# Second layer's lag matrices and phase tables made earlier, decays in two buffers

## Chip, cores and metric

One NeuronCore of a Trainium2 chip runs the whole program. The metric is the device time of one execution in microseconds. The kernel before took 1739.98 us in the median of three runs (1738.82 to 1740.71).

## What is computed

The reference is a trunk of two layers over 528 tokens (16 meta tokens and 512 others) of width 1024. Each layer has a mixer with two branches, and behind it a feed-forward part: dense SwiGLU in the first layer, top-2-of-8 experts in the second. The change touches the S5 branch of the mixer, a diagonal complex recurrence of 64 states for each of 32 groups of 16 channels:

```python
for layer in range(DEPTH):
    z = rmsnorm(hs, mix_norm[layer]) @ w_in[layer]
    # s5_branch: per group 16 inputs drive 64 complex states
    bu = einsum('btgh,gph->btgp', u, bb)          # bb from lambda, dt, B
    s  = associative_scan(s[t] = ab * s[t-1] + bu[t])
    y  = Re(einsum('btgp,ghp->btgh', s, c)) + d * u
    y_a = (gelu(y) * sigmoid(gelu(y) @ w_glu + b)) @ w_proj
    # rglru_branch: conv, gates, a real scan
    hs = hs + (gates0 * y_a + gates1 * y_b) @ w_out[layer]
    hs = hs + (swiglu if layer == 0 else moe_swiglu)(rmsnorm(hs, ffn_norm[layer]))
return rmsnorm(hs, final_norm)
```

## The kernel before

All activations lie feature by token in SBUF. TensorE (PE) multiplies in units: one unit is a 128x1024 slab of weights, split by ScalarE (ACT, `split_hi`) and VectorE (DVE, `split_lo`, tile `wl`) into a high and a low part, so that each product is three matmuls. A mixer has 28 such units for `w_in` (`U_IN`), then those of the GLU, the merge and the output. The order on every engine is written out by hand; engines meet at semaphores.

The S5 recurrence is done in chunks of 8 tokens. The 32 groups go in 8 batches of 4 (`NB`, `GB`), and a batch has three parts, one behind each of three units of `w_in`, from the fourth on (`slot_of`; here P1, P2 and P3):

- P1 (L1841 to L1851) turns the **lag matrices** `m1t` of the batch into the matrices of the chunk. Behind it ACT copies `m1`, and DVE makes `m3` (L1289) and `m2` (semaphore `m2_ready`).
- P2 (L1861) gives each chunk's input to the states, into `side`. Behind it DVE runs the **rotation**: it turns the states by the **phase table** of the batch (`rot`), runs a real scan with the **decays** (L1315, `turned<-decay,rot`), and turns back (`state`, semaphore `rot_ready`).
- P3 (L1868, L1869) gives the batch's outputs from `m3`, `m2` and `state`. It waits for the rotation.

So PE has one unit between P2 and P3 in which DVE must do the rotation, and one unit between P1 and P2.

GpSimd (POOL) makes what DVE and PE need for that. For every batch b of either layer it does, in this order (L608 to L662):

```python
if done:
    pool.wait_ge(p1_done, done)        # P1 of batch b-1
    pool.wait_ge(m2_ready, done)       # m2 of batch b-1
...                                    # fetch pbuf of b+1; lag matrices m1t
if done > 1:
    pool.wait_ge(rot_ready, done - 1)  # rotation of batch b-2
...                                    # phase table: a copy and 24 tensor_tensor
if done:
    pool.wait_ge(rot_ready, done)      # rotation of batch b-1
g.tensor_copy(decay[:, :, 1:NC], col1(mag8)).then_inc(tab_ready, 1)
```

`m1t` and `decay` have one buffer, `phases` and the parameters `pbuf` two. The lag matrices take seven instructions, of which L631, the L537 behind it and L634 are 128x512; the table doubles its columns six times with four `tensor_tensor` each (L653, L537, L655, L656). In the second layer, POOL first waits for the dense part's last residual (`hs_at_norm[2]`, L599), fetches `gw` and `pbuf`, and starts with batch 0. Ahead of that, at the end of the first mixer, it fills two DRAM buffers of the expert part with zeros (`zero`, L590 to L596) and then waits for the whole dense part. The dense part works in units like the mixer's; its tiles `gt`, `ft`, `fh`, `fl` are written by ACT and DVE.

In the second mixer, units of the gates need only 512 tokens. At two places of each mixer (`PAIR_AT`) DVE has in addition the RG-LRU's products and scans on 128x1056 tiles (`ii`, `xc`, `th`, `gg`), behind the rotations of batches 3 and 6.

## Time and profile before

| | us |
|---|---|
| median of three runs | 1739.98 |
| profiled execution, its own time | 1742.03 |
| its span | 1740.4 |
| PE busy | 1645.2 (95%) |
| VectorE busy | 1021.3 (59%) |
| ScalarE busy | 778.3 (45%) |
| GpSimd busy | 371.8 (21%) |
| mean granted TensorE clock | 0.977 of full |

The span is that of the profiled execution, from its first to its last instruction; what lies around it is 1.6 us. Stages by the timeline: first mixer to about 355 us, dense part to 796 us, second mixer to about 1140 us, router and experts behind it. A time in a profile row is counted from the span's start; the number behind it is how long the row's instructions took, and what stands in brackets is how long the engine had been idle and who released it.

### The profile page before, as it was taken

The page shows a single profiled execution, that of the slowest core. Times are in us where ns is not written, and L with a number is a line of the kernel's source. Part 1 is how long each engine was busy: PE and PEld are TensorE (multiplying, and loading weights), DVE is VectorE, ACT ScalarE, POOL GpSimd, SP SyncE. Part 2 cuts the span into 40 slices and gives each one's busy share as a digit, 9 for nine tenths or more (in the row PEclk, how much of TensorE's full clock was granted, in tenths as well). Part 3 has the DMA queues.
Part 4 walks back from the last instruction along what each step waited for, and adds up shares of the span by engine and source line. Part 5 has one row for each costly group of instructions (what it writes and reads, how often), then busy time and mean ns, then how long its engine had stood idle before and what let it go on. Part 6 is the DMA issues. An engine that isn't in the chain of part 4 may idle for free. (4 is left out here: it accounts for less than half of the span.)

```text
span 1740.4 us, 26958 instructions
## 1 busy us (share of the span) xinstructions
PE 1645.2 (95%) x10652; PEld 1466.3 (84%) x10652; DVE 1021.3 (59%) x1286; ACT 778.3 (45%) x947; POOL 371.8 (21%) x662
## 2 busy tenths in 40 slices
PE   5899999989999999998999999979999999999992
PEld 5799999989999999998987878757788777777872
DVE  6868477443333233324766676368547766866985
ACT  4354473332221222223353563247446755755773
POOL 7688630020000000004677700020000000000001
PEclk9899999989999999998999999989999999999996
DMA  4522224373232232324532234069658967966994
GB/s 162 119 82 89 82 80 134 99 291 109 84 97 85 86 95 85 96 86 145 115 91 81 83 99 153 13 247 411 245 185 297 339 236 245 376 243 229 369 371 159
DMA packets 99444, 291.24 MB, mean 167 GB/s; under 512 B 27376, under 2 KB 27504, under 8 KB 99200
## 3 DMA queue, kind: packets, MB, share of 16 engines
q1 hardware_dynamic: 84624, 245.43, 41.8%
q0 software_dynamic: 9504, 33.60, 5.4%
q10 hardware_dynamic: 5200, 10.64, 1.9%
q8 instruction: 75, 1.23, 0.3%
q14 instruction: 41, 0.34, 0.1%
HBM read 261.39 MB, written 28.24 MB: 166 GB/s over the span
## 5 line engine op out<-in xcount | busy, mean ns | idle before, releaser
L1157 DVE TENSOR_TENSOR mwl<-mraw,mwh 128x1024 fp32r<-128x1024 f32 x288 | 337.8, 1220 | 73.1 <-ACT mwh L1052 72.1
L1743 PE MATMUL acc<-xh,wh 128*128 128x264 f32 (+1 forms) x1560 | 368.1, 306 | 3.4 <-DVE xl L1157 1.8
L1743 PE MATMUL acc<-xl,wh 128*128 128x264 f32 (+1 forms) x1560 | 360.3, 301 | 0.0
L1743 PE MATMUL acc<-xh,wl 128*128 128x264 f32 (+1 forms) x1560 | 359.3, 300 | 0.0
L1157 DVE TENSOR_TENSOR wl<-raw,wh 128x1024 fp32r<-128x1024 f32 x164 | 203.6, 1242 | 206.0 <-ACT wh L744 205.6
L1052 ACT ACTIVATE mwh<-mraw 128x1024 fp32r<-128x1024 f32 x288 | 288.5, 1053 | 61.9 <-PE acc L2014 32.8
L1743 PEld LDWEIGHTS acc<-xh,wh 128*128 128x128 f32 x1560 | 251.2, 189 | 17.2 <-issue 3.3
L1743 PEld LDWEIGHTS acc<-xl,wh 128*128 128x128 f32 x1560 | 250.2, 189 | 8.7
L1743 PEld LDWEIGHTS acc<-xh,wl 128*128 128x128 f32 x1560 | 249.7, 189 | 9.3
L744 ACT ACTIVATE wh<-raw 128x1024 fp32r<-128x1024 f32 x164 | 172.5, 1052 | 153.1 <-PE acc L1743 149.6
L2012 PE MATMUL acc<-mwh,xth 128*128 128x512 f32 x432 | 171.3, 396 | 7.9 <-ACT ytok L1118 5.4
L2013 PE MATMUL acc<-mwh,xtl 128*128 128x512 f32 x432 | 168.9, 391 | 0.0
L2014 PE MATMUL acc<-mwl,xth 128*128 128x512 f32 x432 | 168.8, 391 | 0.0
L701 POOL DMA_DIRECT2D yg_d<-ytok x11 | 6.0, 541 | 522.3 <-ACT ytok L1118 518.6
L2012 PEld LDWEIGHTS acc<-mwh,xth 128*128 128x128 f32 x432 | 81.5, 189 | 27.3 <-DVE mwl L1157 6.5
L2014 PEld LDWEIGHTS acc<-mwl,xth 128*128 128x128 f32 x432 | 81.4, 189 | 17.5
L2013 PEld LDWEIGHTS acc<-mwh,xtl 128*128 128x128 f32 x432 | 81.6, 189 | 16.4
L601 POOL DMA_DIRECT2D gw<-in_wg x2 | 1.1, 546 | 425.5 <-DVE hs L1411 425.5
L2012 PE MATMUL acc<-mwh,hth 128*128 128x512 f32 x216 | 85.9, 398 | 0.0
L2014 PE MATMUL acc<-mwl,hth 128*128 128x512 f32 x216 | 84.3, 390 | 0.0
L2013 PE MATMUL acc<-mwh,htl 128*128 128x512 f32 x216 | 84.2, 390 | 0.0
L1743 PE MATMUL acc<-fh,wh 128*128 128x264 f32 x384 | 78.8, 286 | 0.0
(412 smaller groups left out, 2661.4 us busy)
## 6 DMA issues: line engine op xcount, KB each, us to landing
mraw<-in_W SPq DMA_DIRECT2D x288, 512.0 KB, 5.6
raw<-in_W SPq DMA_DIRECT2D x164, 512.0 KB, 3.5
xg_d<-zero POOLq DMA_DIRECT2D x15, 512.0 KB, 9.9
yg_d<-ytok POOLq DMA_DIRECT2D x9, 512.0 KB, 4.9
xt<-xg_d POOLq DMA_DIRECT2D x8, 512.0 KB, 8.1
pbuf<-in_s5m POOLq DMA_DIRECT2D x16, 192.0 KB, 3.1
yg_d<-zero POOLq DMA_DIRECT2D x5, 512.0 KB, 20.9
hs<-in_xT SPq DMA_DIRECT2D x8, 264.0 KB, 8.2
```

What stands on the lines that cost most here:

```text
L601: pool.dma_start(gw[:, r, :, :], wg[l, :, r, :, :]).then_inc(wg_landed, 16)
L701: pool.dma_start(rows(yg_d, BASE[ORDER[b]] + t * TOK, n), ytok[0:n, (tb + t) % 2, :])\
L744: a.activation(wh[s][:, :], raw[s][:, :], ACT.Copy).then_inc(hi_ready[s], 1)
L1052: a.activation(mwh[w][:, :], mraw[j % RAWS][:, :], ACT.Copy).then_inc(wide_hi, 1)
L1157: return v.tensor_tensor(out, a, b, op)
L1743: ins = mm(out, w, x[:, t0:t1], start=first and i == 0, stop=last and i == 2)
L2012: mm(out, hi, mwh[w][:, cols], start=first, stop=False)
L2013: mm(out, lo, mwh[w][:, cols], start=False, stop=False)
L2014: return mm(out, hi, mwl[w][:, cols], start=False, stop=last)
```

## The change

- **Second layer, batches 0 and 1**: their lag matrices, phase tables and decays are made during the dense part, behind the writes of zeros, in tiles that are idle then (`early_m1t`, `early_phase`, with work tiles and a small fetch `early_pbuf` of their own). PE and DVE read these tiles for the two batches (`lags_of`, `phase_of`). `pbuf` of both batches is still fetched after the dense part, since P1 and `m2` need the rest of it; PE waits for it, and for the zeros in `tapsT`, at P1 of these two batches.
- **Second layer, batches 2 and 3**: their tables are made at the second mixer's start and behind `m2` of batch 0, ahead of their lag matrices.
- **Second layer, batches 4 to 7**: table b starts as soon as the rotation of b-2 is done, ahead of the lag matrices of b, which still wait for P1 and `m2` of b-1.
- **Decays** are in two buffers, in a place of their own; decays b wait for the rotation of b-2 and not of b-1.
- **First layer**: the order stays lags, table, decays; only the decays' wait for the rotation of b-1 goes.

The core of the diff:

```diff
@@ placements @@
-        decay = place("decay", [P, GB, NC], at=f)
+        f = [LR()[0] + 4 * 12 * T, LR()[1]]
+        early_phase = [place(f"early_phase{b}", [P, 2, GB, NC], at=f) for b in range(2)]
+        f = [LR()[0] + 4 * 3 * T, LR()[1]]
+        early_m1t = [place("early_m1t0", [P, GB, P], at=f)]
+        f = [LR()[0] + 4 * 4 * T, LR()[1]]
+        early_pbuf = place("early_pbuf", [P, 2, 2, GB * GC], at=f)
+        early_pt1 = place("early_pt1", [P, GB * P], at=f)
+        early_pt2 = place("early_pt2", [P, GB * P], at=f)
+        early_bx = place("early_bx", [P, GB, GC], at=f)
+        early_by = place("early_by", [P, GB, GC], at=f)
+        f = [LR()[0] + 4 * 7 * T, LR()[1]]
+        early_m1t.append(place("early_m1t1", [P, GB, P], at=f))
+        decay = place("decay", [P, 2, GB, NC])
+        def early(l, b):
+            return l and b < 2
+        def lags_of(l, b):
+            return early_m1t[b] if early(l, b) else m1t
+        def phase_of(l, b):
+            return early_phase[b] if early(l, b) else phases[:, b % 2]
...
@@ GpSimd: the loop that goes @@
-            for l in range(LAYERS):
-                if l:
-                    pool.wait_ge(hs_ready, hs_at_norm[1])
-                    link(g.memset(zero[:, :], 0.0))
...
-                    pool.wait_ge(zeroed, ZDMAS * 16)
-                    pool.wait_ge(hs_ready, hs_at_norm[2])
...
-                link(g.memset(phases[:, :, 0, :, 0:1], 1.0))
-                link(g.memset(phases[:, :, 1, :, 0:1], 0.0))
-                link(g.memset(tapsT[:, 0:PADW - P], 0.0))
-                link(g.memset(decay[:, :, 0:1], 0.0))
-                for b in range(NB):
...
-                    pool.wait_ge(pb_landed[b % 2], 16 * (l * NB // 2 + b // 2 + 1))
-                    if done:
-                        pool.wait_ge(p1_done, done)
-                        pool.wait_ge(m2_ready, done)
-                    if 0 < b < NB - 1:
-                        pool.dma_start(pbuf[:, (b + 1) % 2, :, :], s5m[l, b + 1, :, :, :])\
-                            .then_inc(pb_landed[(b + 1) % 2], 16)
...
-                    g.tensor_tensor(m1t[:, :, :].rearrange("p g (j h) -> p g j h", h=GC), by_group(pt1), by_group(pt2),
...
-                    phase = phases[:, b % 2]
-                    if done > 1:
-                        pool.wait_ge(rot_ready, done - 1)
...
-                    pool.wait_ge(m1t_ready, done + 1)
-                    link(g.tensor_copy(phase[:, :, :, 1], turn[:, :, 0, gs]))
...
-                    if done:
-                        pool.wait_ge(rot_ready, done)
...
-                    g.tensor_copy(decay[:, :, 1:NC], col1(mag8)).then_inc(tab_ready, 1)
-                    pool.wait_ge(tab_ready, done + 1)
...
@@ GpSimd: what takes its place @@
+            def lags(l, b):
...
+                p1, p2, x, y = (early_pt1, early_pt2, early_bx, early_by) if early(l, b) else (pt1, pt2, bx, by)
+                bb = (early_pbuf if early(l, b) else pbuf)[:, b % 2, 0:2, :].rearrange("p t (g h) -> p t g h", g=GB)
...
+                g.tensor_tensor(lags_of(l, b)[:, :, :].rearrange("p g (j h) -> p g j h", h=GC), by_group(p1), by_group(p2),
+                                ALU.add).then_inc(m1t_ready, 1)
+                pool.wait_ge(m1t_ready, n + 1)
+            def phase_table(l, b):
...
+                p1, p2 = (early_pt1, early_pt2) if early(l, b) else (pt1, pt2)
+                phase = phase_of(l, b)
...
+                link(g.tensor_copy(phase[:, :, :, 1], turn[:, :, 0, gs]))
...
+                    link(g.tensor_tensor(phase[:, 1, :, k:k + c], z1[:, 1, :, :], z2[:, 0, :, :], ALU.add))
+            def decays(l, b):
+                n = l * NB + b
+                gs = slice(l * GROUPS + b * GB, l * GROUPS + (b + 1) * GB)
+                g.tensor_copy(decay[:, b % 2, :, 1:NC], mag8[:, gs].unsqueeze(2).to_broadcast([P, GB, NC - 1]))\
+                    .then_inc(tab_ready, 1)
+                pool.wait_ge(tab_ready, n + 1)
+            def free_batch(l, b):
+                pool.wait_ge(p1_done, l * NB + b)
+                pool.wait_ge(m2_ready, l * NB + b)
+                if 0 < b < NB - 1:
+                    pool.dma_start(pbuf[:, (b + 1) % 2, :, :], s5m[l, b + 1, :, :, :])\
+                        .then_inc(pb_landed[(b + 1) % 2], 16)
+            def unit_phases(phase):
+                link(g.memset(phase[:, 0, :, 0:1], 1.0))
+                link(g.memset(phase[:, 1, :, 0:1], 0.0))
+            link(g.memset(decay[:, :, :, 0:1], 0.0))
+            for b in range(2):
+                unit_phases(phases[:, b])
+            link(g.memset(tapsT[:, 0:PADW - P], 0.0))
+            for b in range(NB):
+                pool.wait_ge(pb_landed[b % 2], 16 * (b // 2 + 1))
+                if b:
+                    free_batch(0, b)
+                lags(0, b)
+                if b > 1:
+                    pool.wait_ge(rot_ready, b - 1)
+                phase_table(0, b)
+                decays(0, b)
+            pool.wait_ge(hs_ready, hs_at_norm[1])
+            for b in range(2):
+                pool.dma_start(early_pbuf[:, b, :, :], s5m[1, b, :, 0:2, :]).then_inc(early_landed, 16)
+            link(g.memset(zero[:, :], 0.0))
+            for z in range(0, SLOTS, P):
+                n = min(P, SLOTS - z)
+                pool.dma_start(xg_d[z:z + n, :], zero[0:n, :]).then_inc(zeroed, 16)
+            for z in range(FIRST_EXTRA, SLOTS, P):
+                n = min(P, SLOTS - z)
+                pool.dma_start(yg_d[z:z + n, :], zero[0:n, :]).then_inc(zeroed, 16)
+            pool.wait_ge(zeroed, ZDMAS * 16)
+            pool.wait_ge(early_landed, 16 * 2)
+            pool.wait_ge(rot_ready, NB)
+            for b in range(2):
+                lags(1, b)
+                unit_phases(early_phase[b])
+                phase_table(1, b)
+                decays(1, b)
+            pool.wait_ge(hs_ready, hs_at_norm[2])
+            for r in range(2):
+                pool.dma_start(gw[:, r, :, :], wg[1, :, r, :, :]).then_inc(wg_landed, 16)
+            for b in range(2):
+                pool.dma_start(pbuf[:, b, :, :], s5m[1, b, :, :, :]).then_inc(pb_landed[b], 16)
+            g.memset(tapsT[:, 0:PADW - P], 0.0).then_inc(taps_zeroed, 1)
+            for b in range(2):
+                unit_phases(phases[:, b])
+            phase_table(1, 2)
+            free_batch(1, 1)
+            phase_table(1, 3)
+            for b in range(2, NB):
+                n = NB + b
+                if b > 3:
+                    pool.wait_ge(rot_ready, n - 1)
+                    phase_table(1, b)
+                pool.wait_ge(rot_ready, n - 1)
+                decays(1, b)
+                pool.wait_ge(pb_landed[b % 2], 16 * (NB // 2 + b // 2 + 1))
+                free_batch(1, b)
+                lags(1, b)
...
@@ VectorE, TensorE @@
-                        phase = phases[:, b % 2]
+                        phase = phase_of(l, b)
...
-                        link(v.tensor_tensor_scan(flat(turned), flat(decay), flat(rot), 0.0, ALU.mult, ALU.add))
+                        link(v.tensor_tensor_scan(flat(turned), flat(decay[:, b % 2]), flat(rot), 0.0, ALU.mult, ALU.add))
...
+                        lag = lags_of(l, b)
+                        if early(l, b):
+                            pe.wait_ge(pb_landed[b], 16 * (NB // 2 + 1))
+                            pe.wait_ge(taps_zeroed, 1)
```

The change moves instructions on POOL alone. Its rows at two places follow, as the programs have them, with the semaphores that each waits for. First the end of the first mixer's work: before, POOL goes from the writes of zeros (`zero`) to the fetches that wait for the dense part's end (`gw`, `pbuf`).

```order
L590 MEMSET zero 128x1024 [waits hs_ready,tab_ready]
L593 DMA xg_d<-zero 128x1024 [waits pool_chain]
L593 DMA xg_d<-zero 128x1024 x14
L596 DMA yg_d<-zero 128x1024 x5
L601 DMA gw<-in_wg 128x512 [waits hs_ready,zeroed]
L601 DMA gw<-in_wg 128x512
L603 DMA pbuf<-in_s5m 128x384 x2
L604 MEMSET phases 128x2x4
```

Now, from the writes of zeros on, the first lag matrices of the second layer follow, behind `zeroed` (`early_pt_113` and `early_pt_114` are the work tiles `early_pt1` and `early_pt2`):

```order
L696 DMA early_pbuf<-in_s5m 128x128 [waits hs_ready,tab_ready]
L696 DMA early_pbuf<-in_s5m 128x128
L697 MEMSET zero 128x1024
L700 DMA xg_d<-zero 128x1024 [waits pool_chain]
L700 DMA xg_d<-zero 128x1024 x14
L703 DMA yg_d<-zero 128x1024 x5
L621 TENSOR_TENSOR early_pt_113<-cfr,early_pbuf 128x128 [waits rot_ready,early_landed,zeroed]
L562 TENSOR_TENSOR early_pt_113<-cfi,early_pbuf 128x128
L623 TENSOR_TENSOR early_bx<-early_pt_113 128x64 [waits pool_chain]
L562 TENSOR_TENSOR early_by<-early_pt_113 128x64
L629 TENSOR_TENSOR early_pt_113<-apr,early_bx 128x512 [waits pool_chain]
L562 TENSOR_TENSOR early_pt_114<-api,early_by 128x512
```

Two fetches stand ahead of the zeros, and everything for batches 0 and 1 stands between the zeros and the fetch of `gw`.

Then the second layer around batch 5, whose lag matrices are the `m1t` row. Before, the two rows on top end the table of batch 4, the decays are those of batch 4, and the last row starts the table of batch 5:

```order
L655 TENSOR_TENSOR phases<-pt_85,pt_86 128x4x2 [waits pool_chain]
L656 TENSOR_TENSOR phases<-pt_85,pt_86 128x4x2
L661 COPY decay<-mag_143 128x4x65 [waits rot_ready,pool_chain]
L620 DMA pbuf<-in_s5m 128x384 [waits p1_done,m2_ready,pb_landed1,tab_ready]
L623 TENSOR_TENSOR pt_85<-cfr,pbuf 128x128
L537 TENSOR_TENSOR pt_85<-cfi,pbuf 128x128
L625 TENSOR_TENSOR bx<-pt_85 128x64 [waits pool_chain]
L537 TENSOR_TENSOR by<-pt_85 128x64
L631 TENSOR_TENSOR pt_85<-apr,bx 128x512 [waits pool_chain]
L537 TENSOR_TENSOR pt_86<-api,by 128x512
L634 TENSOR_TENSOR m1t<-pt_85,pt_86 128x512 [waits pool_chain]
L643 COPY phases<-turn 128x8 [waits m1t_ready,rot_ready]
```

Now the two rows on top end the table of batch 5, the decays are those of batch 5, and the last row starts the table of batch 6:

```order
L656 TENSOR_TENSOR phases<-pt_84,pt_85 128x4x2 [waits pool_chain]
L657 TENSOR_TENSOR phases<-pt_84,pt_85 128x4x2
L663 COPY decay<-mag_151 128x4x65 [waits rot_ready,pool_chain]
L672 DMA pbuf<-in_s5m 128x384 [waits p1_done,m2_ready,pb_landed1,tab_ready]
L621 TENSOR_TENSOR pt_84<-cfr,pbuf 128x128
L562 TENSOR_TENSOR pt_84<-cfi,pbuf 128x128
L623 TENSOR_TENSOR bx<-pt_84 128x64 [waits pool_chain]
L562 TENSOR_TENSOR by<-pt_84 128x64
L629 TENSOR_TENSOR pt_84<-apr,bx 128x512 [waits pool_chain]
L562 TENSOR_TENSOR pt_85<-api,by 128x512
L632 TENSOR_TENSOR m1t<-pt_84,pt_85 128x512 [waits pool_chain]
L644 COPY phases<-turn 128x8 [waits rot_ready,m1t_ready]
```

Between two sets of lag matrices there is one table as before, but it is the next batch's table; the lag matrices stay behind the same `p1_done` and `m2_ready`.

## Rows read from the trace of the kernel before

**Rows 1.** Waits: engine, line, waited for; us in total, times, longest.

```profile
PE side L1868 <- DVE state L1157: 9.2, 5, 3.5
DVE rot L1157 <- POOL decay L661: 3.7, 5, 1.3
```

**Rows 2.** Timeline of PE, second mixer, batches 2, 4 and 7: start, us, instruction.

```profile
884.12 1.00 PE L1861 MATMUL side<-uu,m 128*128 128x66 f32 x8
...
890.60 0.33 PE L1868 MATMUL side<-uu,m 128*128 128x66 f32 x2
...
898.93 0.63 PE L1841 MATMUL side<-m1t,pbuf 128*32 128x128 f32 x8
...
928.81 1.00 PE L1861 MATMUL side<-uu,m 128*128 128x66 f32 x8
...
938.41 0.69 PE L1868 MATMUL side<-uu,m 128*128 128x66 f32 x2 [2.98 <-DVE state L1157]
...
949.91 0.63 PE L1841 MATMUL side<-m1t,pbuf 128*32 128x128 f32 x8
...
1001.82 1.00 PE L1861 MATMUL side<-uu,m 128*128 128x66 f32 x8
...
1009.49 0.44 PE L1868 MATMUL side<-uu,m 128*128 128x66 f32 x2 [1.04 <-DVE state L1157]
```

**Rows 3.** Windows: stretch, length, PE busy (matmuls), granted clock, DMA share, GB/s.

```profile
172.00:174.00 2.00, 2.00 (x16) 1.00 0.68 170
939.00:945.00 6.00, 6.00 (x23) 0.51 0.35 98
```

**Rows 4.** Timeline of PE, first mixer, batches 0 and 4.

```profile
72.32 0.70 PE L1868 MATMUL side<-uu,m 128*128 128x66 f32 x2 [3.51 <-DVE state L1157]
...
170.46 0.44 PE L1868 MATMUL side<-uu,m 128*128 128x66 f32 x2 [1.49 <-DVE state L1157]
```

**Rows 5.** Timeline of DVE, second mixer: end of rotation 3, rotation 4.

```profile
912.41 0.48 DVE L1157 TENSOR_TENSOR state<-state,rot 128x260 f32<-128x260 f32 x1
...
929.44 1.23 DVE L1157 TENSOR_TENSOR wl<-raw,wh 128x1024 fp32r<-128x1024 f32 x1
931.47 1.32 DVE L1157 TENSOR_TENSOR rot<-side,phases 128x264 f32<-128x264 f32 x3 [0.79 <-POOL decay L661]
...
934.56 2.39 DVE L1157 TENSOR_TENSOR rot<-turned,phases 64x260 f32<-64x260 f32 x2
936.98 1.37 DVE L1157 TENSOR_TENSOR state<-state,rot 128x260 f32<-128x260 f32 x1
```

**Rows 6.** Timeline of POOL, second mixer: table and decays 4, lags 5, table 5.

```profile
910.61 0.43 POOL L643 COPY phases<-turn 128x8 f32<-128x8 f32 x1
...
930.96 0.40 POOL L661 COPY decay<-mag 128x260 f32<-128x260 f32 x1
...
934.28 1.18 POOL L631 TENSOR_TENSOR pt<-apr,bx 128x512 f32<-128x512 f32 x1
...
936.74 1.32 POOL L634 TENSOR_TENSOR m1t<-pt,pt 128x512 f32<-128x512 f32 x1
938.20 0.21 POOL L643 COPY phases<-turn 128x8 f32<-128x8 f32 x1
...
947.91 0.40 POOL L661 COPY decay<-mag 128x260 f32<-128x260 f32 x1
```

**Rows 7.** Timeline of DVE, second mixer, rotation of batch 7, first and last step.

```profile
1005.11 1.32 DVE L1157 TENSOR_TENSOR rot<-side,phases 128x264 f32<-128x264 f32 x3 [0.63 <-POOL decay L661]
...
1009.01 0.43 DVE L1157 TENSOR_TENSOR state<-state,rot 128x260 f32<-128x260 f32 x1
```

**Rows 8.** Timelines of the dense part: DVE, then ACT, then POOL's next instruction.

```profile
399.76 1.23 DVE L1157 TENSOR_TENSOR wl<-raw,wh 128x1024 fp32r<-128x1024 f32 x1 [3.56 <-ACT wh L744]
404.13 0.70 DVE L1157 TENSOR_TENSOR ft<-gt,acc 128x528 f32<-128x528 f32 x1 [3.15 <-PE acc L1743]
```

```profile
409.92 0.61 ACT L977 ACTIVATE gt<-acc 128x528 f32<-128x528 f32 x1 [3.20 <-PE acc L1743]
```

```profile
796.17 1.08 POOL L601 DMA_DIRECT2D gw<-in_wg  x2 [425.47 <-DVE hs L1411]
```

84 lines of the change are left out of this document (36 added, 48 removed).

## The prediction

> **What bounds the kernel now.** PE is the engine that sets the time, so I read its waits first. In the S5 parts only one wait of PE has a cost: P3 waits for DVE's rotation, five times, 9.2 us in all, and DVE waits for POOL's decays five times, 3.7 us in all [rows 1]. PE's timeline says where the five are. In the first mixer 3.51 us (batch 0) and 1.49 us (batch 4) [rows 4], in the second 2.98 us (batch 4) and 1.04 us (batch 7) [rows 2]; that leaves 9.2 - 9.02, some 0.2 us, for the fifth. Nowhere does PE wait for lag matrices.
>
> The windows add a second cost. In the 6 us behind the wait of 2.98 us the granted clock is 0.51, near the lower of its two levels (1.2 and 2.4 GHz) [rows 3]. Behind the wait of 1.49 us it is 1.00 [rows 3]. So one long pause has a price that goes on after it.
>
> Then I follow the chain from P3 back. In batch 4 of the second mixer DVE has ended its weight split at 929.44 + 1.23 = 930.67, and starts the rotation only at 931.47, 0.79 us later, released by the decays [rows 5]. The decays come at 930.96 because they stand behind a table that took from 910.61 to 930.96, 20.35 us [rows 6]. The next table took 947.91 - 938.20 = 9.71 us [rows 6]. The slow one ran beside the long RG-LRU instructions of DVE. In batch 7, behind the second set of these, the rotation too is released by the decays, 0.63 us late [rows 7].
>
> **What each stall costs.** From P2 to P3 batch 2, which does not wait, needs 890.60 - 884.12 = 6.48 us; from P3 to the next P1 it needs 898.93 - 890.60 = 8.33 us [rows 2].
> - Batch 4, P2 to P3: 938.41 - 928.81 = 9.60, so 3.12 us too long [rows 2].
> - Batch 4, P3 to P1 at the lower clock: 949.91 - 938.41 = 11.50, so 3.17 us too long [rows 2]. It is the same sequence of matrices: P3, one gate product, one unit.
> - Batch 7, P2 to P3: 1009.49 - 1001.82 = 7.67, so 1.19 us too long [rows 2].
>
> Together 7.48 us can be had in the second mixer.
>
> **The change part by part.**
>
> *Tables a batch ahead, decays in two buffers (batches 4 to 7).* Table b starts when rotation b-2 is done; its decays are then ready a whole batch before they are used. DVE's waits of 0.79 and 0.63 us go. In batch 4 that alone is not enough: from its start to its end that rotation took 936.98 + 1.37 - 931.47 = 6.88 us [rows 5], against 1009.01 + 0.43 - 1005.11 = 4.33 us in batch 7 [rows 7]. The late part of it is long: two instructions of 64 partitions took 2.39 us and the last one 1.37 us against 0.43, while POOL ran L631 and L634 of 128x512 (934.28, 936.74) [rows 5, 6]. By the shorter duration the rotation would run from 930.7 to 935.0, and P3 can start at 928.81 + 6.48 = 935.3 [rows 2]. So the question is what POOL does between 930.7 and 935. Table 5 starts now at 912.9, when rotation 3 ends [rows 5], 2.3 us later than table 4 did, beside the same RG-LRU instructions. If it also takes 20.35 us it ends at 933.3; then come the decays (0.4), and L631 starts as long after them as before, 934.28 - 931.36 = 2.9 us, that is at 936.6, behind the rotation's end. Small table instructions may still hold up some of DVE's. The nearest bounds for what is left of the wait: below, 0 (the rotation ends 0.3 us early); above, all of the old stretch, 6.88 - 4.33 = 2.55 us, less these 0.3, that is 2.3 us. I take 0.4 us, near the lower end, since L631 to L634 no longer fall into the rotation by this reckoning.
>
> With so short a wait the clock stays up: 1.49 us of waiting did not lower it, 2.98 us did [rows 2 to 4]. So 3.17 us go as well.
>
> In batch 7 POOL has no table left to make while the RG-LRU runs, DVE is free at 1004.5 or earlier, and the rotation ends at 1004.5 + 4.33 = 1008.8 at the latest, while P3 could start at 1001.82 + 6.48 = 1008.3. The earlier it is, the more the last 0.5 us go too: DVE's work ahead of it no longer collides with POOL's. I count the full 1.19 us, and keep 0.7 as the other end.
>
> *What is late next.* The lag matrices of 5 now stand behind table 5. They took 938.06 - 931.36 = 6.7 us from the decays' end [rows 6], so they are ready at about 933.7 + 6.7 = 940.4; P1 of batch 5 comes at 949.91 - 3.12 - 3.17 = 943.6. There are 3.2 us to spare, and this is the tightest place. POOL's fetch of `pbuf` for batch 6 moves with the lag matrices and has a batch's time.
>
> *Batches 0 and 1 made early.* Two sets of lag matrices (6.7 us each at most) and two tables with decays (9.71 + 0.4 us) are some 34 us of POOL, plus four memsets and two fetches of 64 KB. They fall into the 425 us in which POOL is idle [rows 8]. PE did not wait for these matrices or tables before, so this part gives nothing by itself; it makes room at the second mixer's start. Its price is DVE held up in the dense part. Units there end 409.92 - 404.13 = 5.8 us apart; the split that ends at 400.99 belongs to the unit that starts at 409.9 [rows 8]. With 8.9 us of cover, a hold of 1.3 us (L634, [rows 6]) costs nothing; if that cover were gone, each one that falls on a split would cost up to 1.3 us. The two new waits of PE at P1 of batches 0 and 1 are for a fetch and a memset that are issued right after the dense part, ahead of all units of the mixer. I count 0.
>
> *First layer.* Order and waits stay but for the decays' wait, and there the table ends last. Its waits of 3.51 and 1.49 us [rows 4] remain. Two more small memsets at its start are hidden. 0 us.
>
> **The sum.** 3.12 + 3.17 + 1.19 - 0.4 = 7.1 us less. The profiled execution took 1742.03 us, so 1734.9 on its own account. It stands 2.05 us above the median of 1739.98. I take the same step from the median: **1732.9 us**. The four times known spread over 1738.82 to 1742.03, 3.2 us, which is about one fall of the clock. If the median run had none, the gain from it is 3.9 us only, 1736.1.
>
> **The rivals.**
> 1. *The lag matrices still hit the rotation of batch 4.* Table 5 may be quicker than table 4, or DVE later, and then L631 to L634 fall into it as before. For it: they follow the same `m2_ready`, and the collision is seen [rows 5, 6]. Against it: the later start of the table. The rotation would end at 930.7 + 6.88 = 937.6, PE waits 2.3 us. That lies between 1.49 and 2.98, so the clock may hold or fall: 0.8 + 1.2 + 3.2 = 5.2 us less (1734.8) or 2.0 less (1738.0). The Trainium skill (SBUF — State Buffer, Who interferes with whom) says that a VectorE instruction with two SBUF inputs and a GpSimd instruction that reads SBUF exclude each other, the later one blocking until the other is through; the trace agrees, with 1.37 against 0.43 us [rows 5, 7]. By that rule moving POOL's work removes no conflict, it only chooses which DVE instruction meets it.
> 2. *The tables are not ahead where it counts, or the median runs have other stalls*: 1740, no change. Against it: both waits named by the decays [rows 5, 7].
> 3. *The dense part pays.* DVE is held up beside 34 us of POOL work and PE starves now and then, 3 to 4 us in all: 1736 to 1737. Against it: 8.9 us of cover.
> 4. *Slower: lag matrices 5 late for P1.* If every one of the table's 25 instructions had to wait out a DVE instruction as long as a split, 1.23 us [rows 5], it would take 30.8 us, and with decays and lag matrices `m1t` would come at 912.9 + 30.8 + 7.1 = 950.8. From 943.6 on each microsecond is PE's: 7.2 us of wait, and the clock falls again (3.2). Less the 7.1 gained, that is 3.3 us slower, 1743.3; with lag matrices held up as well, 1745. It turns to a loss from an `m1t` of about 947.5 on. Against it: the slow table took 20.35 us beside the same instructions.
>
> **How the numbers follow.** A difference of 0.2%, 3.5 us, is about what a measurement of this kernel can tell from none. The forecast, 1731 to 1736.1: 0.66, faster. Rival 1: 0.15, of which 0.08 faster and 0.07 within. Rival 2: 0.07, within. Rival 3: 0.07, within. Rival 4: 0.05, slower. That makes 0.74 faster, 0.21 the same, 0.05 slower. The range goes from 1731.0 (nothing left of any wait, and a little relief of DVE elsewhere) to 1739.0, which takes in rival 1 with the clock's fall and rival 3.
>
> **What the changed profile would show.** P2 to P3 of batches 4 and 7 at 6.5 to 6.9 us; no window of low clock behind batch 4; no DVE wait for decays in the second mixer; POOL at work for some 34 us soon after the writes of zeros, with PE still at full pace; P1 of batch 5 without a wait. I am wrong if P1 waits for `m1t`, if PE has gaps in the dense part, or if rotation 4 is still as long as 6.9 us.

## The result and the profile after

| | us |
|---|---|
| before, median of 12 runs beside the change | 1741.63 |
| after, median of 12 runs | 1737.71 (1735.23 to 1743.62) |
| ratio after/before, 95% interval | 0.9979 (0.9969 to 0.9988) |
| profiled execution, before and after | 1742.03 and 1738.40 |
| its span, before and after | 1740.4 and 1736.9 |

Faster, but by half of what was forecast: 3.6 us between the two profiled executions and 3.9 us between the medians, where the sum said 7.1. The time of 1737.71 lies in the range, near its upper end. Ratios here and below are those on record; they are not the quotients of the two medians, which differ from them by up to 0.0006. Two runs far off the others, 2731.53 us of the kernel before and 5660.8 us of the run "tables ahead alone" (mean granted clock 0.56 and 0.27), count in the medians and not in the ratios.

The signs that the prediction named are there: no low clock behind batch 4, no wait for decays in the second mixer, POOL at work from 397.28 to 430.61 us (33.3 us, forecast some 34), P1 of batch 5 without a wait. None of the three that were to show it wrong came: P1 does not wait for `m1t`, rotation 4 takes 4.43 us (930.07 to 934.50), and from 372 to 797 us PE has one wait of 1.1 us, which it had before. The loss is elsewhere. PE's timeline of the second mixer, after, batches 4, 5 and 7 (L1936 is P2, L1943 P3, L1877 the gate product, L1916 P1; start, us, instruction, in brackets idle time and who ended it):

```profile
928.67 1.00 PE L1936 MATMUL side<-uu,m 128*128 128x66 f32 x8
...
935.12 0.33 PE L1943 MATMUL side<-uu,m 128*128 128x66 f32 x2
...
943.46 0.63 PE L1916 MATMUL side<-m1t,pbuf 128*32 128x128 f32 x8
...
951.80 1.00 PE L1936 MATMUL side<-uu,m 128*128 128x66 f32 x8
...
959.64 0.44 PE L1943 MATMUL side<-uu,m 128*128 128x66 f32 x2 [1.24 <-DVE state L1228]
...
961.48 1.64 PE L1877 MATMUL side<-xc,gw 128*128 128x264 f32 x4
...
969.68 0.52 PE L1916 MATMUL side<-m1t,pbuf 128*32 128x128 f32 x6
...
998.45 1.00 PE L1936 MATMUL side<-uu,m 128*128 128x66 f32 x8
1004.92 0.33 PE L1943 MATMUL side<-uu,m 128*128 128x66 f32 x2
```

Against [rows 2]: P2 to P3 of batch 4 takes 6.45 us in place of 9.60, P3 to P1 8.34 in place of 11.50, P2 to P3 of batch 7 6.47 in place of 7.67. All three stalls of the sum are gone in full. (The forecast for the two P2 to P3 was 6.5 to 6.9 us.) P1 of batch 5 does not wait. But batch 5, which had no stall before, now has one: P2 to P3 takes 7.84 us, 1.36 too long, and P3 to P1 10.04, 1.7 too long.

The waits of the whole execution after, to set beside [rows 1], show 2.6 us less of PE's waiting for rotations: the waits of 2.98 and 1.04 us are gone, one of 1.24 us is new, and one in the first mixer grew to 0.18. The three waits for decays that are left are the first mixer's:

```profile
PE side L1943 <- DVE state L1228: 6.6, 5, 3.5
...
DVE rot L1228 <- POOL decay L663: 2.3, 3, 1.3
```

The windows after, in the columns of [rows 3] (here with the busy time of PE's weight load, VectorE, ScalarE and GpSimd between PE and the clock), show where the clock is low: no longer behind batch 4, but behind batch 5.

```profile
939.00:945.00 6.00, 6.00 (x38) 4.52 (x37) 1.85 (x1) 1.49 (x3) 5.31 (x16) 1.00 0.44 112
961.00:966.00 5.00, 5.00 (x19) 4.07 (x19) 0.00 (x0) 3.19 (x5) 4.38 (x17) 0.66 0.47 128
```

So the time from P2 of batch 4 to P3 of batch 7 fell from 80.68 us (1009.49 - 928.81) to 76.25 (1004.92 - 928.67), by 4.43: 3.15 + 3.16 + 1.20 gained, 1.36 + 1.70 lost in batch 5, the rest rounding.

What made rotation 5 late stands in two timelines. VectorE, after, rotation 5:

```profile
952.84 1.32 DVE L1228 TENSOR_TENSOR rot<-side,phases 128x264 f32<-128x264 f32 x3 [2.12 <-PE side L1936]
954.19 0.43 DVE L1228 TENSOR_TENSOR rot<-rot,rot 128x264 f32<-128x264 f32 x1
954.66 1.45 DVE L1386 TENSOR_TENSOR_SCAN turned<-decay,rot 128x264 f32<-128x264 f32 x1
956.14 1.11 DVE L1228 TENSOR_TENSOR state<-turned,phases 128x260 f32<-128x260 f32 x1
957.27 1.86 DVE L1228 TENSOR_TENSOR rot<-turned,phases 64x260 f32<-64x260 f32 x2
959.16 0.43 DVE L1228 TENSOR_TENSOR state<-state,rot 128x260 f32<-128x260 f32 x1
```

GpSimd, after: table 5 and its decays, lag matrices 5 (their last step), table 6 and its decays, lag matrices 6:

```profile
912.88 1.09 POOL L644 COPY phases<-turn 128x8 f32<-128x8 f32 x1 [2.50 <-DVE state L1228]
...
933.65 0.57 POOL L663 COPY decay<-mag 128x260 f32<-128x260 f32 x1
...
939.16 1.29 POOL L632 TENSOR_TENSOR m1t<-pt,pt 128x512 f32<-128x512 f32 x1
940.51 1.07 POOL L644 COPY phases<-turn 128x8 f32<-128x8 f32 x1
...
951.47 0.40 POOL L663 COPY decay<-mag 128x260 f32<-128x260 f32 x1
952.17 0.58 POOL L672 DMA_DIRECT2D pbuf<-in_s5m  x1 [0.30 <-POOL decay L663]
...
954.30 1.25 POOL L629 TENSOR_TENSOR pt<-apr,bx 128x512 f32<-128x512 f32 x1
955.51 1.46 POOL L562 TENSOR_TENSOR pt<-api,by 128x512 f32<-128x512 f32 x1
957.04 1.36 POOL L632 TENSOR_TENSOR m1t<-pt,pt 128x512 f32<-128x512 f32 x1
```

The rotation took 6.75 us, with four instructions held up beside the three of 128x512 on POOL. Before, lag matrices 6 waited 7.13 us for `m2` of batch 5, and their first step (956.04) began 3.2 us ahead of the rotation (959.28):

```profile
955.44 0.58 POOL L620 DMA_DIRECT2D pbuf<-in_s5m  x1 [7.13 <-DVE m L1157]
956.04 0.42 POOL L623 TENSOR_TENSOR pt<-cfr,pbuf 128x128 f32<-128x128 f32 x1
```

Now `m2` of batch 5 is done at 949.31, but POOL comes out of decays 6 only at 951.87, and starts the lag matrices with the rotation (952.77 and 952.84). Table 5 was slow (20.8 us beside the RG-LRU), so lag matrices 5 were late, so table 6, which now stands ahead of lag matrices 6, ended late.

The dense part, after, on POOL and VectorE; the early lag matrices of batch 0 hold up one weight split, 2.14 us in place of 1.23 [rows 8], and the next `ft` comes at its time (404.19, before 404.13). Those of batch 1 hold up another, 2.20 us at 418.77.

```profile
399.82 1.06 POOL L562 TENSOR_TENSOR early_pt<-api,early_by 128x512 f32<-128x512 f32 x1
400.96 2.16 POOL L632 TENSOR_TENSOR early_m1t<-early_pt,early_pt 128x512 f32<-128x512 f32 x1
```

```profile
399.82 2.14 DVE L1228 TENSOR_TENSOR wl<-raw,wh 128x1024 fp32r<-128x1024 f32 x1 [3.56 <-ACT wh L815]
404.19 0.70 DVE L1228 TENSOR_TENSOR ft<-gt,acc 128x528 f32<-128x528 f32 x1 [2.23 <-PE acc L1814]
```

### The profile page after: what moved, and what is told of

Its sections match the earlier page's. It is cut to its first block, busy times and chain, and to the rows that moved or that the text cites. A ratio compares the mean times of both kernels' runs of the same rounds, so it can differ in the third digit from the quotient of the medians.

```text
span 1736.9 us, 26954 instructions
## 1 busy us (share of the span) xinstructions
PE 1641.1 (94%) x10652; PEld 1462.4 (84%) x10652; DVE 1022.5 (59%) x1286; ACT 778.3 (45%) x947; POOL 358.5 (21%) x671
## 3 DMA queue, kind: packets, MB, share of 16 engines
q8 instruction: 75, 1.23, 0.3%
## 4 chain that ended last, share of the span: by engine, by line
PE 83%; DVE 6%; issue 4%; DMA 3%; POOL 2%; ACT 1%; POOLq 0%; ACTq 0%; SPq 0%; DVEq 0%
PE acc L1814 45%; PE acc L2087 7%; PE acc L2089 7%; PE acc L2088 7%; PE side L1814 4%; PE acc L1857 2%; PE acc L2085 2%; DMA mraw<-in_W 2%; PE acc L2086 2%; DVE rot L1228 1%; PE side L1943 1%; PE side L1877 1%; PE side L1944 1%; PE side L2133 1%; PE side L1936 1%
## 5 line engine op out<-in xcount | busy, mean ns | idle before, releaser
L1814 PE MATMUL acc<-fl,wh 128*128 128x264 f32 x384 | 78.3, 285 | 0.0
```

The costliest lines, as they stand in the source:

```text
L1814: ins = mm(out, w, x[:, t0:t1], start=first and i == 0, stop=last and i == 2)
```

## The experiments

**Theories.** 1, collision: what is missing from the gain is the wait and the clock in batch 5, caused by lag matrices 6 running beside rotation 5. 2, lost behind the mixer: the expert blocks, bound by their weight DMA, swallow part of what the mixer gains. 3, the early work costs something in the dense part. In the diffs, `lags`, `phase_table` and `decays` are the calls of the second layer's loop on POOL.

### Lag matrices 6 ahead of table 6

```diff
             for b in range(2, NB):
                 n = NB + b
+                if b in (6,):
+                    pool.wait_ge(pb_landed[b % 2], 16 * (NB // 2 + b // 2 + 1))
+                    free_batch(1, b)
+                    lags(1, b)
                 if b > 3:
                     pool.wait_ge(rot_ready, n - 1)
                     phase_table(1, b)
                 pool.wait_ge(rot_ready, n - 1)
                 decays(1, b)
-                pool.wait_ge(pb_landed[b % 2], 16 * (NB // 2 + b // 2 + 1))
-                free_batch(1, b)
-                lags(1, b)
+                if b not in (6,):
+                    pool.wait_ge(pb_landed[b % 2], 16 * (NB // 2 + b // 2 + 1))
+                    free_batch(1, b)
+                    lags(1, b)
```

> The change, but in batch 6 of the second mixer POOL makes the lag matrices ahead of the table. Theory 1 (collision): in the change the lag matrices of 6 stand behind table 6 and start at 952.8 with rotation 5, which takes 6.8 us in place of 4.3; PE then waits 1.24 us and its clock falls (1.7 us more). Here they start at about 950, when m2 of batch 5 is ready, rotation 5 takes 5.0 to 5.8 us, the wait at P3 of batch 5 is under 0.4 us, no granted clock under 0.9 follows, and P3(5) to P3(6) is shorter by 2.5 to 3 us. Mixer end 2.5 to 3 us ahead of the change's; median 1734.5 to 1735.5 against the change's 1737.7. Theory 2 (what is gained in the mixer is lost again in the expert blocks, whose weight DMA is the bound): the mixer gains as said, but the end moves by under 1 us, 1737. Rival (the wait at batch 5 comes from RG-LRU work of DVE or from the P2 side, not from POOL): the wait of 1.24 us stays.

Measured: 1736.73 us (1734.16 to 1739.82, 12 runs), ratio to before 0.9978 (0.9968 to 0.9987). Rotation 5 takes 4.57 us, P3 of batch 5 does not wait, and from P2 of batch 5 to P2 of batch 6 it takes 22.24 us, in the change 25.32 (977.12 - 951.80): 3.08 us back. The window in which the change's clock was 0.91:

```profile
960.00:980.00 20.00, 20.00 (x104) 16.12 (x104) 10.47 (x19) 11.37 (x15) 18.17 (x45) 1.00 0.32 99
```

P3 of batch 7 waits anew, 0.91 us: table 7 pushes lag matrices 7 beside VectorE's second set of RG-LRU instructions, of which three take 2.0 to 2.2 us in place of 1.26. So the order of POOL's work makes the stall of batch 5. The time did not follow as forecast: the median lies 1.0 us under the change's, not 2.5 to 3, and the ratio to before is 0.9978 where the change's was 0.9979, so this run alone shows no gain over the change; see the repeats below.

### Lag matrices 5 and 6 ahead of their tables

The same edit with `(5, 6)`.

> As the run before, and in batch 5 too the lag matrices come ahead of the table. Theory 1: lag matrices 5 then run from about 927.5 to 933 and meet rotation 4 (930.1) 2.6 us into them; by the same offset rotation 3 of the change took 5.4 us, so rotation 4 takes some 5.3 in place of 4.4 and P3(4) waits for up to 0.5 us. Table 5 moves off the RG-LRU instructions of DVE and takes about 10 us in place of 20. Total within 0.7 us of the run before, 1734.5 to 1736. If the two RG-LRU hold-ups of DVE by table 5 cost PE anything, this run is faster than the run before by more than 0.7 us.

Measured: 1739.33 us (1736.42 to 1741.57, 11 runs), ratio 0.9987 (0.9978 to 0.9996). Batch 5 as in the run before, but P3 of batch 4 now waits 0.70 us, and that batch takes 24.09 us from P2 to P2 in place of 23.12. Lag matrices 5 ran their 128x512 steps from 932.40 to 936.3, rotation 4 from 931.78 to 937.95, 6.2 us. Table 5, off the RG-LRU, took 10.5 us (936.39 to 946.89) and bought nothing. The collision goes where the lag matrices go. The forecast of a time within 0.7 us of the run before was missed, by 2.6 us of median. A second thing showed up: the first mixer, whose code is the same in both, was 2.0 us longer in this profile, 1.6 of them in batch 4, where its clock fell behind the wait.

### The early part alone

```diff
-            phase_table(1, 2)
             free_batch(1, 1)
-            phase_table(1, 3)
             for b in range(2, NB):
                 n = NB + b
-                if b > 3:
-                    pool.wait_ge(rot_ready, n - 1)
-                    phase_table(1, b)
-                pool.wait_ge(rot_ready, n - 1)
-                decays(1, b)
                 pool.wait_ge(pb_landed[b % 2], 16 * (NB // 2 + b // 2 + 1))
                 free_batch(1, b)
                 lags(1, b)
+                pool.wait_ge(rot_ready, n - 1)
+                phase_table(1, b)
+                pool.wait_ge(rot_ready, n)
+                decays(1, b)
```

> The change's early lag matrices and tables of batches 0 and 1 alone: batches 2 to 7 in the old order (lag matrices, table, then decays once the rotation before is done). Theory 1 and my forecast (the early part gives nothing by itself, and costs nothing): batch 4 waits 3 us for the rotation and the clock falls, batch 7 waits 1 us, time as before, 1741 to 1742. Theory 3 (the early work costs something in the dense part): slower than before, 1743 or more, and the dense part begins or ends later than in the kernel before by over 1 us. If the early part by itself brings POOL ahead, the waits shrink and the time falls under 1740.

Measured: 1742.35 us (1741.43 to 1747.6, 12 runs) beside 1741.08 for before, ratio 1.0009 (1.0000 to 1.0018). Batch 4 takes 29.58 us from P2 to P2, before 29.43 (958.24 - 928.81), and P3 of batch 7 waits 1.01. From the last norm of the first mixer's output to the last norm of the dense part's (PE's products with `ones` behind `hn`, 357.49 and 794.36 us; before, 357.99 and 794.77) it took 436.87 us, before 436.78. So the early part gives nothing by itself, and no cost of it above 0.1 us is seen in the profile; the interval of the ratio leaves room for up to 0.18%.

### Tables ahead alone

The early part undone: `early` always returns False, and in the second mixer batches 0 and 1 are made at its start:

```diff
-                return l and b < 2
+                return False
...
-            phase_table(1, 2)
-            free_batch(1, 1)
-            phase_table(1, 3)
+            for b in range(2):
+                pool.wait_ge(pb_landed[b], 16 * (NB // 2 + 1))
+                if b:
+                    free_batch(1, 1)
+                lags(1, b)
+                phase_table(1, b)
+                decays(1, b)
...
-                if b > 3:
+                if b > 1:
```

> The change without its early part: in the second mixer batches 0 and 1 are made at their old place, tables a batch ahead and decays in two buffers from batch 2 on. Theory 1: table 2 and 3 come later, but POOL has 4 to 7 us of idle time per batch, so by batch 4 it has caught up: mixer as in the change (gain of 4 to 5 us at its end), 1737 to 1738.5. If the early part is needed (makes room at the start of the mixer), batch 2 or 3 stalls: P3 waits of 1 us or more there, and 1740 or more. Theory 3 (early work costs something in the dense part) expects this kernel to be faster than the change, by 1 us or more.

Measured: 1738.36 us (11 runs; ten lie from 1736.12 to 1742.39), ratio 0.9982 (0.9970 to 0.9994). P1 of batch 2 waits 0.99 us and P3 of batch 3 1.27 us, batches 1 to 3 take 2.2 us more than before from P2 to P2; so the early part does make room. Theory 3 had this kernel faster than the change, and it is not (the change's ratio was 0.9979). Batch 5 has the change's collision, and the very same wait:

```profile
964.92 0.44 PE L1941 MATMUL side<-uu,m 128*128 128x66 f32 x2 [1.24 <-DVE state L1226]
```

Behind it, in the window that follows, the granted clock stays up:

```profile
966.00:972.00 6.00, 6.00 (x32) 5.06 (x32) 0.01 (x1) 4.42 (x7) 5.21 (x19) 1.00 0.43 112
```

Batch 5 takes 23.74 us here and 25.32 in the change: 1.6 us apart, by the clock alone. But the first mixer's clock fell here, behind the wait of batch 4 that other executions pass at full clock. So a wait of this size does not by itself fix what the clock does.

### The change again, and lag matrices 6 held back

The change unaltered, the run with lag matrices 6 first once more, and a third way on one chip. The third keeps the change's order and only holds lag matrices 6 back until rotation 5 is through:

```diff
                 free_batch(1, b)
+                if b == 6:
+                    pool.wait_ge(rot_ready, n)
                 lags(1, b)
```

> The change itself, unaltered, on the same chip as the next three runs. P3 of batch 5 again waits 1.24 us for rotation 5, since that is fixed by the order of POOL's work. Theory 1 (whether the clock falls behind such a wait is not set by the wait's length, but differs from run to run: the same wait of 1.5 us in the first mixer's batch 4 lowered it in two of six profiles, and the same wait of 1.24 us in batch 5 lowered it in the change and not in the kernel without the early part): the fall behind it may be there (period from P2 of batch 5 to P2 of batch 6: 25.3 us) or not (23.7 us). Rival (a wait of this length in this place always lowers the clock): 25.3 us again. Median 1737 to 1738.5.

> The kernel of the run lags6_first once more, beside the change on one chip, to compare the two. Theory 1: period of batch 5 at 22.24 us again; median lower than the change's by between 1.3 us (the wait alone, if most runs keep the clock up) and 3 us (if most runs of the change lose the clock too). Theory 2 (lost again behind the mixer): equal medians within 0.5 us.

> The change, in its own order (table 6, decays, lag matrices 6), but POOL holds lag matrices 6 back until rotation 5 is done: one wait more and no work moved ahead of other work. Theory 1 (collision on the port): rotation 5 takes 4.3 to 4.5 us in place of 6.8, P3 of batch 5 does not wait, the period of batch 5 is 22.2 to 22.3 us; lag matrices 6 end about 962.5, 4 us before P1 of batch 6 at about 966.6, so nothing else waits; same time as lags6_again within 0.5 us. Rival (the wait at batch 5 was caused by the decays or the table, or by DVE's own order): the wait of 1.24 us stays. If DVE is then held up elsewhere by the later lag matrices, the next weight split is late and PE waits for wl.

| kernel | median us | runs | ratio to before (1742.66) |
|---|---|---|---|
| the change | 1737.65 | 6 | 0.9966 (0.9954 to 0.9978) |
| lag matrices 6 first | 1736.34 | 5 | 0.9959 (0.9946 to 0.9973) |
| lag matrices 6 held | 1735.80 | 5 | 0.9956 (0.9943 to 0.9970) |

The held kernel adds a wait and no more, and the stall of batch 5 is gone. VectorE's rotation 5, and POOL beside it:

```profile
951.12 1.32 DVE L1230 TENSOR_TENSOR rot<-side,phases 128x264 f32<-128x264 f32 x3 [2.12 <-PE side L1938]
952.47 0.43 DVE L1230 TENSOR_TENSOR rot<-rot,rot 128x264 f32<-128x264 f32 x1
952.94 0.71 DVE L1388 TENSOR_TENSOR_SCAN turned<-decay,rot 128x264 f32<-128x264 f32 x1
953.69 0.43 DVE L1230 TENSOR_TENSOR state<-turned,phases 128x260 f32<-128x260 f32 x1
954.13 0.86 DVE L1230 TENSOR_TENSOR rot<-turned,phases 64x260 f32<-64x260 f32 x2
955.03 0.43 DVE L1230 TENSOR_TENSOR state<-state,rot 128x260 f32<-128x260 f32 x1
```

```profile
955.55 1.30 POOL L621 TENSOR_TENSOR pt<-cfr,pbuf 128x128 f32<-128x128 f32 x1 [4.50 <-DVE state L1230]
...
960.12 1.29 POOL L632 TENSOR_TENSOR m1t<-pt,pt 128x512 f32<-128x512 f32 x1
```

The scan takes 0.71 us in place of 1.45, the pair of 64 partitions 0.86 in place of 1.86, the rotation 4.34 in place of 6.75; batch 5 takes 22.24 us. That shows theory 1. Lag matrices 7 then fell into rotation 6 (P3 waits 1.31 us, the clock stays at 1.00 behind it). The unaltered change fell again behind its 1.24 us, 25.36 us for batch 5.

From P2 of batch 4 to P3 of batch 7 the change took 76.33 us here, lag matrices 6 first 74.25 and held 74.75, so 2.1 and 1.6 us less (the 3.1 of batch 5, less the new stall of batch 7 or 6). The medians are 1.3 and 1.9 us under the change's, on five and six runs, and the intervals of the three ratios overlap; what shows the gain is the stretch in the profiles.

### First mixer: tables ahead too

```diff
             for b in range(NB):
+                if b in (4, 5, 7):
+                    pool.wait_ge(rot_ready, b - 1)
+                    phase_table(0, b)
+                    decays(0, b)
                 pool.wait_ge(pb_landed[b % 2], 16 * (b // 2 + 1))
...
                 lags(0, b)
-                if b > 1:
-                    pool.wait_ge(rot_ready, b - 1)
-                phase_table(0, b)
-                decays(0, b)
+                if b not in (4, 5, 7):
+                    if b > 1:
+                        pool.wait_ge(rot_ready, b - 1)
+                    phase_table(0, b)
+                    decays(0, b)
```

on top of lag matrices 6 first.

> The kernel of lags6_first, and in the first mixer too the tables of batches 4, 5 and 7 come a batch ahead (table, decays, lag matrices). Theory 1: rotation 4 of the first mixer no longer waits for its decays nor runs beside lag matrices 5, so the wait of 1.5 us at P3 of batch 4 goes, and with it the fall of the clock that follows it in some runs (1.65 us); but table 4 now pushes lag matrices 4 back into rotation 3, 1.5 us or so longer, of which P3(3) waits 0.5 us at most, with a wait of that size seldom lowering the clock. Net 1 us faster than lags6_again in runs that kept the clock, up to 2.7 in the others: median 1735 to 1735.7. If the collision of rotation 3 is worse (offset as in rotation 5 of the change), P3(3) waits 1.2 us and the gain is nil.

Measured: 1738.51 us (1736.29 to 1742.14, 8 runs), 2.2 us slower than lag matrices 6 first on the same chip; its profiled run took 1742.14. The aim was met: batch 4 no longer waits for its rotation and takes 24.06 us from P2 to P2, 25.87 in lag matrices 6 first. Rotation 3 takes 4.48 us, no collision. But table 4, made first, put lag matrices 4 beside the RG-LRU; their last step ended at 154.44, and P1 was there first:

```profile
152.35 2.09 POOL L632 TENSOR_TENSOR m1t<-pt,pt 128x512 f32<-128x512 f32 x1
```

```profile
154.53 0.63 PE L1926 MATMUL side<-m1t,pbuf 128*32 128x128 f32 x8 [1.77 <-issue]
```

```profile
150.00:164.00 14.00, 12.22 (x77) 11.04 (x76) 13.55 (x16) 6.11 (x9) 13.31 (x18) 0.76 0.32 103
```

The wait and the clock behind it cost that stretch 4.9 us (28.01 from P2 of batch 3 to P2 of batch 4 in place of 23.13). In batch 6 lag matrices 7 then fell into the rotation, and P3 waits 1.02 us (23.54 in place of 22.23). This is rival 4 of the prediction, in the other mixer: I had not expected it here.

### Once more on one chip, lag matrices 7 first as well, and pauses made on purpose

> The change, unaltered, a third profile, on the same chip as the next runs. P3 of batch 5 waits 1.24 us; the period of batch 5 is 25.3 us if the clock falls behind it and 23.7 if it holds. Median 1737 to 1738.5.

> The kernel of lags6_held once more. Period of batch 5 at 22.24 us, P3 of batch 6 waits 1.3 us since lag matrices 7 now fall into rotation 6. Theory 1: median 1.3 to 2 us under the change's of the same call. Theory 2 (what the mixer gains is lost behind it): within 0.5 us.

> As lags6_first, and in batch 7 too the lag matrices come ahead of the table. In lags6_again table 7 ended at 975.3 and pushed lag matrices 7 beside DVE's second set of RG-LRU instructions; DVE was 0.7 us late and P3 of batch 7 waited 0.92 us. Here lag matrices 7 start with m2 of batch 6 at about 971.5, 2.4 us ahead of rotation 6, which costs under 1 us of its slack; table 7 then runs beside the RG-LRU instructions and takes up to 20 us, to about 997, and its decays are the risk. Theory 1: if table 7 is done by 996, neither P3(6) nor P3(7) waits, mixer end 0.5 to 1 us ahead of lags6_again, median 1735 to 1736. If it takes the full 20 us, rotation 7 waits for the decays as in the kernel before, about 1 us, and nothing is gained.

| kernel | median us | runs | ratio to before (1742.15) |
|---|---|---|---|
| the change | 1737.87 | 12 | 0.9981 (0.9970 to 0.9992) |
| lag matrices 6 held | 1736.45 | 6 | 0.9966 (0.9954 to 0.9978) |
| lag matrices 6 and 7 first | 1736.33 | 7 | 0.9967 (0.9955 to 0.9980) |

The change's batch 5 took 25.36 us once more, the other two 22.24. With lag matrices 6 and 7 first, P3 of batch 7 still waits, 1.02 us: table 7 beside the RG-LRU instructions ran from 977.65 to 998.18, 20.5 us, and the rotation was released by its decays 0.63 us late, as in the kernel before. That is the second of the two outcomes that were written down for it.

The kernel with pauses is lag matrices 6 first, with dead work on VectorE that was to make P3 wait where nothing collides:

```diff
+                        for _ in range({2: 5, 5: 4, 6: 5}.get(b, 0) if l else 0):
+                            link(tt(rot[:, :, :], phase[:, 0, :, :], phase[:, 1, :, :], ALU.mult))
                         tt(state[:, :, new], state[:, :, new], swapped[:, :, new], ALU.add).then_inc(rot_ready, 1)
```

> The kernel of lags6_first, with five, four and five dependent dead multiplications of 128x264 (0.43 us each, their result is not used) put ahead of the last instruction of rotations 2, 5 and 6 in the second mixer, so that P3 waits there though nothing collides. Each wait is the added time (2.2 to 2.6 us, in batch 5 1.8 to 2.1) less the slack of 0.6 to 1.1 us: 1.1 to 1.9 us. Theory 1 (a wait of this size lowers the clock in some places and runs and not in others): not all three waits and the one of 1.5 us in the first mixer have the same outcome, or the outcome does not go by length. Rival (a threshold of length between 1 and 3 us): the longer ones fall, the shorter ones don't, without exception. A fall costs 1.5 to 1.7 us each time it lasts 3.4 us.

Measured (one execution, 1752.20 us): waits of 2.03, 0.93 and 3.88 us in batches 2, 5 and 6, and 1.53 in the first mixer. None of the three lies in the forecast 1.1 to 1.9: in batch 2 a rotation instruction took 1.32 us in place of 0.43 beside a 128x512 step, and in batch 6 the five dead instructions took 3.99 us in place of 2.30 (batch 2), beside lag matrices 7. The windows behind batches 2, 5 and 6:

```profile
896.00:902.00 6.00, 6.00 (x23) 5.10 (x22) 3.30 (x4) 3.56 (x5) 5.48 (x14) 0.53 0.25 55
...
968.00:974.00 6.00, 6.00 (x35) 5.20 (x34) 0.75 (x1) 3.77 (x6) 5.47 (x15) 1.00 0.39 110
995.00:1001.00 6.00, 6.00 (x25) 5.06 (x25) 5.42 (x6) 3.71 (x4) 0.00 (x0) 0.72 0.13 36
```

The longest wait was not followed by the longest fall: behind 2.03 us the clock was at 0.53 over its window, behind 3.88 us at 0.72. Over all profiles the outcome goes by length only at the ends:

| wait of P3, us | profiles and places | clock fell |
|---|---|---|
| 0.70 to 1.04 | 10, batches 4 to 7 of either mixer | 0 of 10 |
| 1.24 | batch 5 of the change three times, of tables ahead once | 3 of 4 |
| 1.27 to 1.32 | batch 3 of tables ahead, batch 6 of held, twice | 0 of 3 |
| 1.49 to 1.57 | first mixer's batch 4 in 13 profiles, same code but for the decays' wait of before | 3 of 13 |
| 2.0 to 3.9 | batch 4 of before and of the early part alone, two of the pauses | 4 of 4 |

(The first mixer's batch 0 is left out, since PE has other pauses ahead of it. Waits of P1 are not in the table: 1.77 us of first mixer, tables ahead, after which the clock fell, and 0.99 us of tables ahead alone, after which it did not.)

## Why the prediction was wrong

**Where PE stalls, and what each stall costs: right.** 3.12, 3.17 and 1.19 us were to be had and were had: 3.15, 3.16, 1.20. The 0.4 us kept back in batch 4 was not lost.

**Table 5 and decays 5: right.** It took 912.88 to 933.6, forecast 912.9 to 933.3. `m1t` of batch 5 was done at 940.45, forecast 940.4, and P1 came at 943.46, forecast 943.6. That 940.4 is so close is luck in part: the decays ended 0.5 us later than forecast (934.22) and the lag matrices took 6.2 us and not 6.7.

**"What is late next": the step that failed.** I followed the lag matrices of 5 to their consumer P1 and stopped there, calling it the tightest place. I did not follow POOL itself one batch further. After `m1t` 5 at 940.4 comes table 6, 9.71 us by [rows 6], then 0.4 us of decays; that is 950.5 (measured 951.87), and lag matrices 6 start then, no longer when `m2` of batch 5 is ready. Their first 128x512 step comes 2.9 us later, at 953.4 (measured 954.30). Rotation 5 starts 9.4 us after P1 of batch 5 (in the kernel before, 959.28 - 949.91), so at 953.0 (measured 952.84). Every number of this could be had from the trace of before. The sum has no term for it, and it cost 1.36 us of wait and 1.70 us of clock. Rival 1 was the right mechanism, set against the wrong batch: I asked whether the lag matrices still hit rotation 4, and they hit rotation 5. The scan of rotation 5 took 1.45 us beside POOL's 128x512 steps and 0.71 without them. That these steps are the cause is shown by moving them, ahead of the rotation or behind it: both times batch 5 takes 22.24 us. The Trainium skill (SBUF — State Buffer, Who interferes with whom) says that a VectorE instruction with two SBUF inputs and a GpSimd one that reads SBUF exclude each other; the inference drawn from it beside rival 1, that moving POOL's work only chooses which instruction is met, told this outcome better than the sum did.

**"With so short a wait the clock stays up": wrong as a rule.** It rested on one wait of 1.49 and one of 2.98 us. The sum used it only where no wait was left, so it did no harm in batch 4. In batch 5 a wait of 1.24 us was followed by a fall in three of four profiles, which cost 1.6 to 1.7 us each time; behind the 1.5 us of the first mixer it fell in 3 of 13.

**Batches 0 and 1 early: no gain by itself, right; no cost, as far as seen.** PE ran without a gap beside this work. That it "makes room" is shown: without it batches 1 to 3 lose 2.2 us. The two weight splits that it held up, by 0.9 and 1.0 us, fit the cover of 8.9 us that the prediction counted on.

**The step from mixer to median.** The sum carried the mixer's gain to the end unchanged. Against the profile of before, three profiles of the change were 4.5 us ahead over the second mixer; from 1150 to 1210 us, router and first expert block, they gave back 0.8, 1.5 and 1.5 us, the five of lag matrices 6 first, 6 held, and 6 and 7 first -0.1 to 0.9, but first mixer, tables ahead 2.7 and the pauses 1.8, both with batch 5 free of the collision too. There the mean busy share of the DMA engines is 1.02 to 1.03, and the change gave back time although its granted clock was the higher one (1.00 against 0.83 from 1150 to 1180 us). Two waits for `hb`, the experts' hidden values, total 4.6 us in the change, before there is one of 1.5. Theory 2 holds in that small part. What decides between 0 and 2.7 is open, and no run tested it.

**The sum as it should have stood:** 7.48 - 1.36 - 1.70 = 4.4 us less in the mixer, up to 1.5 of it given back in the change's profiles, so 2.9 to 4.4; the medians are 3.9 apart. The other part of the miss in microseconds is the base: the three runs that I had gave 1739.98 for before and twelve give 1741.63, so the step of 2.05 us from the profiled execution down to the median should have been 0.4. Together 3.2 us of missing gain and 1.65 of base make the 4.8 us between 1732.9 and 1737.71.

## What to carry to other kernels

When work is moved ahead on an engine that runs its list in order, follow that engine for at least one more round than the change touches. Check each later piece against what it runs beside, not only against who waits for it. Where two engines hold each other up, it can pay to make the one with time to spare wait: one added wait here took the rotation from 6.75 to 4.34 us, and the median was lower than the change's in both comparisons, by 1.9 and 1.4 us, with intervals that overlap. Do not set a price on a clock fall from one wait that kept the clock and one that did not; read several profiles of the same code.

## What the runs showed of the chip that I had not expected

- The same wait in the same place (1.24 us; 1.5 us) lowers the granted clock in some executions and not in others. The lower level then lasts 3.4 us or 6.8 us: 0.66 over 5 us, and 0.51 over 6 us with 3.17 us lost. What decides between the two was not tried.
- These falls make much of the scatter between the profiled executions. The start of the dense part has one in every profile, but of two lengths: over 360 to 374 us the granted clock was 0.63 before and 0.76 in two later profiles of the change and of lag matrices 6 held, whose code there is the change's, and at its end (796 to 812 us) 0.68 and 0.79. Each longer one costs some 1.3 us: from P2 of the first mixer's batch 7 to P2 of the second mixer's batch 0 it takes 604.2 us with both long (before), 602.7 with one (lag matrices 6 first, again) and 601.5 with none (lag matrices 6 held). Two such places make 2.6 us of difference between kernels that are equal there, nearly as much as the 3.1 us of batch 5.

```profile
360.00:374.00 14.00, 10.26 (x54) 9.98 (x55) 11.32 (x17) 5.88 (x10) 10.53 (x20) 0.63 0.91 339
796.00:812.00 16.00, 11.78 (x71) 11.23 (x72) 12.52 (x17) 6.05 (x11) 12.91 (x27) 0.68 0.26 89
```

(the kernel before), and lag matrices 6 held:

```profile
360.00:374.00 14.00, 9.88 (x68) 9.33 (x69) 10.96 (x17) 5.82 (x11) 12.60 (x23) 0.76 0.78 284
796.00:812.00 16.00, 12.22 (x82) 11.96 (x79) 13.20 (x19) 6.39 (x10) 12.86 (x34) 0.79 0.22 74
```

- How much a rotation suffers goes by where in it the three 128x512 steps fall. It takes 4.34 us alone; 4.57 where the first step of the lag matrices (L621, before L623) began 3.2 us ahead of it (before, batch 5: 956.04 and 959.28), 5.26 at 3.4 us (after, batch 6), 5.37 at 2.1 us (after, batch 3), 6.17 at 1.8 us (lag matrices 5 and 6 first, batch 4), 6.75 at 0.1 us (after, batch 5). The offset alone does not fix it: 3.2 and 3.4 us differ by 0.7 us of rotation. PE forgives about 1.1 us of it (6.75 - 4.34 = 2.41 us longer, 1.24 us of wait).
